# Forget chain and first loads earlier, prompt rows 20 steps behind the K pages, a new order in the first stage

## The reference, cut to what matters

```python
m = silu(c) @ ada_w + ada_b                     # adaLN: shift, scale, gate; layers 0 and 1
h = rmsnorm(x, pre_g) * (1 + scale) + shift
# layer 0: pooling mixer
u, z = split(h @ in_w)                          # 1024 -> 2 x 2048
mixed = (pooled(u) @ grp_w) * a_scale           # windows 2, 4, 8, 16
x = x + gate * rmsnorm((mixed * silu(z)) @ out_w, post_g)
# shared stream
k, v, f = split(rmsnorm(x, kv_g) @ kv_w);  logf = log_sigmoid(f + f_b)
# layer 1: forgetting attention, 16 heads of 64
F = cumsum(logf)                                # prompt: own rows; sample: 2048 cached rows and 4 new
s = q @ k.T / 8 + F_query - F_key               # causal
x = x + gate * rmsnorm((softmax(s) @ v * silu(zg)) @ b_out_w, post_g)
```

## Time and profile before

| what | us |
|---|---|
| three timed runs | 2025.97, 2026.33, 2029.84; median 2026.33 |
| the profiled execution, its own time | 2030.65 |
| span of its instructions | 2028.9 |
| PE busy | 1814.9 (89%) |
| DVE busy | 843.7 (42%) |
| POOL busy | 608.4 (30%) |
| ACT busy | 512.8 (25%) |

### The profile page before, as it was taken

How to read it: one execution, slowest core, us unless ns; L and a number is a source line. 1 busy time by engine, 2 the same in 40 slices (tenths; PEclk the granted TensorE clock), 3 DMA queues, 4 the chain that set the end, 5 groups by cost and what they waited for, 6 DMA issues and landing times. The chain is left out here.

```text
span 2028.9 us, 31452 instructions
## 1 busy us (share of the span) xinstructions
PE 1814.9 (89%) x12391; PEld 1476.0 (73%) x12391; DVE 843.7 (42%) x1209; ACT 512.8 (25%) x990; POOL 608.4 (30%) x513
## 2 busy tenths in 40 slices
PE   3999799989979899479999999589999999999598
PEld 1899799979966676379999999556556655655276
DVE  2731423406325658612111000277666665665152
ACT  2210100101112221301000011145555544544121
POOL 0523223223228778322222223312111111111150
PEclk9999899999989999789999999789999999999699
DMA  9223223332137444133432322557888988977751
GB/s 312 86 79 104 83 92 119 95 98 70 41 137 252 170 135 146 67 90 109 119 84 77 111 88 87 179 158 255 283 295 314 329 290 280 325 243 249 274 210 67
DMA packets 208077, 334.96 MB, mean 165 GB/s; under 512 B 41769, under 2 KB 142746, under 8 KB 205123
## 3 DMA queue, kind: packets, MB, share of 16 engines
q1 hardware_dynamic: 176140, 286.32, 42.7%
q10 hardware_dynamic: 31791, 46.62, 6.7%
HBM read 287.26 MB, written 45.63 MB: 164 GB/s over the span
## 5 line engine op out<-in xcount | busy, mean ns | idle before, releaser
L136 PE MATMUL ps<-actH,w_hi_a 128*128 128x352 f32 x912 | 201.0, 329 | 19.6 <-POOL w_lo_a L124 19.6
L136 PE MATMUL ps<-actH,w_lo_a 128*128 128x352 f32 x912 | 197.7, 324 | 0.0
L136 PE MATMUL ps<-actL,w_hi_a 128*128 128x352 f32 x912 | 197.5, 325 | 0.0
L136 PE MATMUL ps<-actH,w_hi_c 128*128 128x352 f32 x792 | 173.6, 327 | 15.8 <-DVE w_lo_c L94 15.8
L136 PEld LDWEIGHTS ps<-actH,w_hi_a 128*128 128x128 f32 x912 | 155.4, 190 | 33.3 <-issue 33.3
L136 PE MATMUL ps<-actH,w_lo_c 128*128 128x352 f32 x792 | 171.6, 324 | 0.0
L136 PE MATMUL ps<-actL,w_hi_c 128*128 128x352 f32 x792 | 171.4, 325 | 0.0
L122 POOL CAST w_hi_a<-w_raw_a 128x1024 fp32r<-128x1024 f32 (+1 forms) x48 | 44.1, 920 | 398.0 <-PE ps L136 282.0
L1574 POOL TENSOR_SCALAR diag<-ident,rinv 128x128 f32<-128x128 f32 x128 | 75.9, 605 | 286.6 <-DVE rinv L1850 286.4
L136 PEld LDWEIGHTS ps<-actH,w_lo_a 128*128 128x128 f32 x912 | 157.7, 189 | 0.0
L1655 PE MATMUL ps<-ident,K 128*128 128x128 f32 x1024 | 141.6, 282 | 17.3 <-issue 13.6
(11 more groups left out here) (245 smaller groups left out, 3040.1 us busy)
## 6 DMA issues: line engine op xcount, KB each, us to landing
K<-in_cache_k_dram SPq DMA_DIRECT2D x128, 512.0 KB, 5.8
V<-in_cache_v_dram SPq DMA_DIRECT2D x128, 512.0 KB, 4.9
w_raw_t<-in_a_out_w_dram SPq DMA_DIRECT2D x48, 512.0 KB, 3.6
ada<-in_ada_w_dram SPq DMA_DIRECT2D x16, 1024.0 KB, 6.1
w_raw_a<-in_a_in_w_dram SPq DMA_DIRECT2D x32, 512.0 KB, 4.4
g_d<-g ACTq DMA_DIRECT2D x16, 528.0 KB, 2.7
mov_t<-g_d SPq DMA_DIRECT2D x16, 528.0 KB, 4.5
ada<-in_ada_w_dram SPq DMA_DIRECT2D x16, 512.0 KB, 4.6
```

The costliest lines, as they stand in the source:

```text
L136: mm = pe.matmul(acc[:, c, 0:CH], wt[:, j % SPL, k, :], act[:, k0 + k, c * CH:(c + 1) * CH], start=first and k == 0 and s == 0, stop=last ...
```

## The change

**Entry.** The three vectors are loaded as 40 rows of 128 values and turned by one PE transpose. The last token rows and the history move from ACT's queue to SP's, behind the adaLN loads, and the first two weight jobs move ahead of adaLN block 6. The transposed rounds use four PSUM banks instead of two, strips 0 and 1 of the first two jobs are done as their rounds become ready, and the history is turned between strips 1 and 2. The bias load moves by a table of its own, from right behind the last piece to three jobs later.

```diff
-        BANKS = 2
+        BANKS = (6, 7, 2, 5)
...
+        BIAS_LOAD = {17: 2 * KD + 1, 38: 3 * KD + 2}
...
-                    sp.dma_start(kvg[:, :], kv_g.rearrange("(k p) -> p k", p=P)).then_inc(s_small, 16)
...
+                sp.dma_start(vrow[2 * KD:3 * KD, :], kv_g.rearrange("(k p) -> k p", p=P)).then_inc(s_small, 16)
...
-                        r = PIECE[n + 4]
-                        condition(r)
-                        if items[r][1] == KD - 1:
-                            condition(r + 1)
+                        condition(PIECE[n + 4])
+                    if n in BIAS_LOAD:
+                        condition(BIAS_LOAD[n])
...
+                for m in range(2 * HALF):
+                    c, k = m // HALF, m % HALF
+                    pe.wait_ge(normed.low[m % 2], m // 2 + 1)
+                    for n in range(2):
+                        if m == 0:
+                            pe.wait_ge(w["split"], n + 1)
+                        step(n, c, k)
+                        if n == 0 and m in turns:
+                            normed.pe(pe, x_tok, s_xn, lambda i: i + 1, *turns[m])
+                pe.wait_ge(normed.done, 1)
+                pe.wait_ge(s_hist, 16)
```

```diff
+                    elif j == 30:
+                        sp.wait_ge(s_G, 2)
+                        sp.dma_start(G_d[:, 0:PAST], LT[:, 0:PAST]).then_inc(s_Gd, 16)
...
+                    if LF_TURN <= n < LF_TURN + 2:
+                        turn_forget(2 * (n - LF_TURN))
+                        turn_forget(2 * (n - LF_TURN) + 1)
...
+        PL = UN + 4
...
-                loads.append((UN * p - 20 + 2 * n, what, p))
+                loads.append((PL + UN * p - 20 + 2 * n, what, p))
...
-            loads.append((UN * bq - 8 if bq else 1.0, "B", bq))
+                loads.append((UN * bq - 4, "B", bq))
...
-                for R, c in ((0, 0), (0, 1), (0, 2), (1, 0), (1, 1)):
-                    scores(R, c)
...
                 for s in range(STEPS):
-                    R, k = s // 4, s % 4
+                    R, k = (s - PL) // 4, (s - PL) % 4
...
-                    if R < RN and k < 3:
+                    if now and k < 3:
                         turn_probs(R, k, 0)
```

More of the change, by code:

```diff
@@ L320, in pe, with act @@
             mm.then_inc(self.turned, 1)
-        def act(self, act):
-            for m, k0, A, B, g, k, n in self.parts(0, len(self.rounds)):
+        def act(self, act, lo=0, hi=None):
+            for m, k0, A, B, g, k, n in self.parts(lo, len(self.rounds) if hi is None else hi):
                 act.wait_ge(self.full, m + 1)
@@ L553, in turn_condition, with turn_history @@
                     mm.then_inc(s_mT, 1)
+                def turn_history(m):
+                    if m >= 2:
+                        pe.wait_ge(s_hc, m - 1)
+                    for i in range(4):
+                        j = 4 * m + i
+                        mm = pe.transpose(ps[:, 6 + m % 2, i * NB * HIST:(i + 1) * NB * HIST], hist[:, j * P:(j + 1) * P],
+                                          ident[0:NB * HIST, 0:NB * HIST])
+                    mm.then_inc(s_hT, 1)
                 def finish_tile(j):
@@ L571, in _ @@
                     condition(r)
[L572 to L578, removed]
+                pe.wait_ge(s_small, 48)
+                pe.transpose(ps[:, 5, BANK // 2:BANK // 2 + 3 * KD + KA], vrow[:, :],
+                             ident[0:3 * KD + KA, 0:3 * KD + KA]).then_inc(s_vT, 1)
                 for r in range(4, KD):
@@ L755, in _ @@
                                           ALU.mult).then_inc(s_xn, 1)
+                for q in range(2):
+                    variance(q)
+                    scale_rows(q)
+                dve.wait_ge(s_vT, 1)
+                link(dve, dve.tensor_copy(chan[:, :], ps[:, 5, BANK // 2:BANK // 2 + 3 * KD + KA]))
+                add_bias(0)
+                modulation(0, 0)
+                dve.wait_ge(s_mod, 1)
+                normed.dve(dve, link, 0, 6)
+                variance(2)
+                normed.dve(dve, link, 6, 7)
+                scale_rows(2)
+                normed.dve(dve, link, 7)
                 for m in range(4):
@@ L1220, in _, with turn_forget @@
             @block.tensor
             def _(pe):
+                def turn_forget(i):
+                    pe.wait_ge(s_lfc, 16 * NB * NPG)
+                    if i >= 2:
+                        pe.wait_ge(s_LT, i - 1)
+                    else:
+                        pe.wait_ge(s_lrow, 1)
+                    for g in range(4):
+                        mm = pe.transpose(ps[:, 6 + i % 2, g * P:(g + 1) * P], LF[:, 4 * i + g, :], ident[:, :])
+                    mm.then_inc(s_lT5, 1)
                 late = None
@@ L1590, in _ @@
             def _(pe):
-                for g in range(NPG):
-                    mm = pe.transpose(ps[:, g // 4, g % 4 * P:(g % 4 + 1) * P], LF[:, g, :], ident[:, :])
-                mm.then_inc(s_lT5, 1)
-                pe.wait_ge(s_X, 2)
-                pe.matmul(ps[:, 4, 0:NT], X[:, :, :].rearrange("p b h -> p (b h)"), tsel[:, :],
-                          start=True, stop=True).then_inc(s_newf, 1)
                 def scores(R, c):
```

447 lines of the change are left out of this document (246 added, 201 removed).

## The result

The changed kernel takes 2006.42 us (median of 4 runs, 2004.83 to 2008.02), the kernel before 2027.59 in the same comparison: ratio 0.9895, interval 0.9878 to 0.9912. It is faster by 21 us, where 45 were forecast. One execution among all in this document, of the kernel with a narrow B, ran at a mean granted clock of 0.56 and took 2970.36 us; that kernel's time is given without it.

A forecast was written before the change was run, and what follows sets the result against it. PE bounds most of the program, so gains lie only where it waits or runs at 1.2 GHz. Terms -12.2 - 23.6 + 0.4 - 35.0 + 5 + 20 = -45.4 us give 1985.2 profiled, 1981 median; range 1963 to 2005.

The forecast's parts named there:

- its last line: From profiled execution to timed median: the median stands 4.3 us below, so 1985.2 us becomes 1981.
- the term for steps 22 to 127: Long stretch of the attention loop: same pages and prompt steps, eight more steps with scores to form, +5 us.
- the rivals: Half clock in both thin stretches (0.05), in K stretch alone (0.13); entry head without gain (0.07); stalls that stay (0.03).
- The head of the attention stage: Barrier to step 22: second page at 16.6 us, step 22 at 80.6 us instead of 115.6; -35.0 us.
- the clock's bound: Attention steps 0 to 21: 48 us won at full clock throughout, 17 us at half; 35.0 taken.
- The clock: Rule weighed for the K-page stretch: transposes raise the clock here, by a row, though the Trainium skill says the opposite.
- Both rivals that rested on half clock for the whole stretch: Attention stage: half clock in K stretch alone, 1999 us, chance 0.13; in both thin stretches, 2039 us, chance 0.05.
- The end: Attention step 128 to stage end: 59 us where V pages alone took 39.4, so 20 us given back.
- The slower rival: Attention steps 0 to 21 and 128 to 147: PE's pauses keep the clock at half, 2039 us; chance 0.05.
- The two stalls: Entry stage: moving the bias load ends waits of 10.25 and 9.35 us and 4.0 us of slow clock; -23.6 us.
- The head of the entry stage: Up to the third job: vectors as three small transfers bring the eighth adaLN block to 35.5 us; -12.2 us.
- The projections: Projection stage: added transposes on PE, against an earlier last store and barrier; +0.4 us, between -2 and +4.

The follow-up runs named there:

- the kernel with a narrow B: Changed kernel with B's four loads together in step 12, each only the first 256 of 2,080 columns: 1963.47 us (median of three).
- the kernel with B in quarters: Changed kernel with the four transfers of the forget bias B issued one a step, in steps 12 to 15 of each round: 1969.25 us.
- the trial: Changed kernel with the three entry vector loads, one value per partition, added back on SP's queue into a tile nobody reads: 2007.92 us.
- one experiment here: Changed kernel with the load of B moved from step 12 back to step 8, the prompt's values Vt then behind it: 2007.21 us.
- two more: Prompt rows 8 steps behind the K pages, not 20: on the changed kernel 2008.66 us; with B in quarters, qblk copies and nmask spread, 1969.83 us.

## Why the prediction was wrong

The time is 25.4 us above the forecast. The terms of the sum hold 22.3 of them; the other 3 come from its last line, since the median of the changed kernel lies 1.2 us below its profiled execution and not 4.3.

**The step that failed** is the term for steps 22 to 127, "the same pages, and as many prompt steps", +5 us, measured +20.4. The scores are as priced: in the kernel with B in quarters, at full clock throughout, PE is busy for 443.0 us; before it was 444.7, of which 13.1 us (summed over the stretches at 0.50) ran at half clock and cost 6.5 us extra, so 438.2, and the difference is 4.8. What failed is the wait. The trace of before had it, 2.3 to 3.2 us in five rounds, and the prediction even priced one for the first round ("3 us for a K page that is late behind the load of B, as one is in most rounds of 16 steps now"), but it took the others as unchanged. They were not: 20 steps are a round and four steps, and the change moved the loads of B along with the prompt, from step 8 to step 12 of a round, where PE has 1.2 us less work to cover the page. The waits went from 13.6 to 25.2 us in sum, and the half clock behind them took 25.7 us of PE's busy time instead of 13.1, which is 6.3 us more. 4.8 + 10.2 + 6.3 = 21.3 us, measured 20.4. Put back to step 8 with nothing else in their way, the loads of B leave 14.9 us of waits and 13.7 us at half clock, nearly as before. It could have been read before: in its steps 12 to 14 PE worked 11.7 us (1647.39 to 1659.11 us), in steps 8 to 10, where B was, 13.8.

None of the rivals named a wait that a moved load makes longer. They asked what the clock would do, and whether two waits would go.

**The head of the attention stage** (-35.0, measured -32.4) came near: the second page 16.3 us behind the barrier for 16.6, step 22 83.1 us behind it for 80.6. (The selects end by their own rows at 10.4 + 2.0 = 12.4 us, where 12.2 was taken; DVE began on nmask at 11.6.) Steps with a K page alone took 2.81 us at half clock and 1.97 at full, forecast 2.8 and 1.9. The two ends of the clock's bound both occurred: four pages at 0.50, then full. The late page of step 15 cost 6.3 us, not 3. That steps 1 to 19 took 52 us without this wait, forecast 53 at 2.8 each, is partly luck: steps 5 to 13 took 2.2 us each, as the bound for full clock has it, and steps 1 to 4 and 14 to 19 took 3.2.

**The clock** was weighed by 16 transposes of token tiles, behind which it stood at 1.00. In the loop the four transpositions of K pages alone (1277.7 to 1288.0 us) left it at 0.50; it rose in the first page scores and then stayed up through steps of transposes alone, three in a row at a time (1290.4 to 1310.3 us). The Trainium skill's sentence in "TensorE: Matmul & The Clock Gate", Part 4: PE-mode transpose, that the full clock "doesn't engage" for transposes, agrees with the first half of this and not with the second. Both rivals that rested on half clock for the whole stretch fell.

**The end** (+20, measured +22.7): 62.1 us for 59, at full clock; PE waited 5.7 us for copies of probability blocks, priced at 5. The slower rival, half clock in both thin stretches, needed a mean clock far below the 1.00 in the row.

**The two stalls** (-23.6, measured -23.7) went by their cause: put back, they came back.

**The head of the entry stage** (-12.2, measured -10.6) came near the number, but not by the way told, and that is luck. All of it lies, as the sum had it, ahead of the eighth adaLN block, which was used at 37.8 us, forecast 35.5, before 48.7. But the prediction gave the gain to the loads by single values, at which SP stood for 17.7 us. They hold 3.2 us of it; in the trial SP stood 14 us there again, and meanwhile the transfers had three blocks and token rows to carry. The other 9.0 us came with the place of some 2 MB of token rows and history, which the sum of 12.5 MB had rightly left out without naming it as the gain.

**The projections** (+0.4, measured +1.0) lay within their bounds.

## What to carry to other kernels

When a change shifts one stream of work against another, take every wait that the trace shows in the steady loop and work it out again at the new place: how much work covers the load, and what stands ahead of it in its queue; one experiment here failed by a second load that its edit had put there, and two more stayed open over it. A burst of transfers in front of a small ring of buffers is better cut into pieces over several steps: here what delayed the next page was the burst on the way and not the issuing. An engine's list of preparations ahead of a loop belongs behind the loop's first hand-overs, where it is not needed sooner.

## What the runs showed of the hardware

SP standing at a transfer did not mean that the transfers stood: with SP stuck 14 us at a load by single values the window from 4 to 20 us still moved 365 GB/s (412 without it), as long as transfers issued earlier were left; from 20 to 28 us it was 306 (382). While the four loads of B, packets of 8 KB, were on the way, all transfers together fell to 211 GB/s at a DMA share of 0.82; with an eighth of their bytes, in packets of 1 KB, no K page behind them in steps 22 to 127 waited more than 0.2 us. A wait cost a second time behind it: in the changed kernel the granted clock was 0.50 at each of the six waits of 3.4 to 4.7 us for a K page, 25.7 us of PE's work in all, about half of which is the price. Before the change it was so at three of five waits of 2.3 to 3.2 us.
